# Hybrid decoder step: the sample columns' depthwise convolution moved from 31 small VectorE steps per tile to one GpSimd product and one VectorE sum

## The reference, cut to what matters

```
u = glu[..., :CONV_CH] * sigmoid(glu[..., CONV_CH:])
xx = concatenate([buf, u], 1)            # 30 old positions in front
y = dwconv_valid(xx, w) + b              # y[n] = sum_k w[k] * xx[n + k], k = 0..30
y = silu(layer_norm(y, ln_g, ln_b))
```

## Time and profile before

| | |
|---|---|
| median of 3 runs | 2254.72 us (2253.72 to 2254.95) |
| the profiled execution's own time | 2254.63 us |
| its span | 2252.8 us |
| TensorE matmul busy | 2067.1 us, 92% |
| VectorE busy | 1179.8 us, 52% |
| ScalarE busy | 388.3 us, 17% |
| GpSimd busy | 113.5 us, 5% |

### The profile page before, as it was taken

The page is one execution under the profiler, slowest core; times in us unless marked ns, Lnnn a source line. Parts: engine busy times, 40 slices in busy tenths (PEclk is TensorE's granted clock), DMA queues, the critical chain, the costliest instruction groups (busy, mean ns, idle before and its releaser), DMA issues.

```text
span 2252.8 us, 26851 instructions
## 1 busy us (share of the span) xinstructions
PE 2067.1 (92%) x9950; PEld 1581.3 (70%) x9950; DVE 1179.8 (52%) x3052; ACT 388.3 (17%) x1097; POOL 113.5 (5%) x219
## 2 busy tenths in 40 slices
PE   8998887897999999999999978769979999999999
PEld 6766655675777777777776666547757777777777
DVE  4998365445046776610059983654540567766000
ACT  1012266212110000000000132651120100000000
POOL 1002110000000000000000013000000000000000
PEclk9998688998999999999999986989989999999999
DMA  6103440573211222121231034015622122221121
GB/s 239 68 0 105 142 150 1 163 235 110 83 55 56 78 90 77 38 91 53 88 123 60 0 111 127 1 37 176 201 94 91 47 75 75 75 75 67 52 77 68
DMA packets 109988, 200.27 MB, mean 89 GB/s; under 512 B 13697, under 2 KB 81554, under 8 KB 104610
## 3 DMA queue, kind: packets, MB, share of 16 engines
q1 hardware_dynamic: 103618, 167.01, 22.3%
q0 software_dynamic: 5568, 30.38, 3.8%
q10 hardware_dynamic: 672, 1.16, 0.1%
HBM read 190.81 MB, written 15.94 MB: 92 GB/s over the span
## 4 chain that ended last, share of the span: by engine, by line
PE 84%; DVE 7%; ACT 6%; issue 1%; POOL 1%; DMA 1%; SPq 0%; DVEq 0%; ACTq 0%
PE ps L851 25%; PE ps L528 23%; PE ps L654 9%; PE ps L567 8%; PE ps L541 3%; PE ps L733 2%; PE ps L819 2%; PE ps L918 2%; PE ps L771 1%; ACT rC L1095 1%; ACT rA L1095 1%; PE ps L698 1%; PE ps L639 1%; PE ps L715 1%; ACT rB L951 1%; PE ps L519 1%
## 5 line engine op out<-in xcount | busy, mean ns | idle before, releaser
L528 PE MATMUL ps<-rC,rB 128*128 128x288 f32 x1232 | 300.1, 406 | 0.0
L528 PEld LDWEIGHTS ps<-rC,rB 128*128 128x128 f32 x1232 | 234.1, 190 | 64.7
L1665 DVE TENSOR_TENSOR xT<-xT,ps 128x576 f32<-128x576 f32 x16 | 12.1, 755 | 330.7 <-PE ps L528 294.0
L1294 DVE SCALAR_TENSOR_TENSOR catT<-XC,par,catT 128x512 f32<-128x512 f32 x240 | 180.4, 752 | 8.3
L851 PE MATMUL ps<-catT,rD 128*128 128x288 f32 x528 | 131.6, 406 | 0.0
L528 PE MATMUL ps<-catT,WR 128*128 128x288 f32 x512 | 130.0, 414 | 1.1 <-ACT catT L951 1.1
L654 PE MATMUL ps<-WR,rD 128*128 128x254 f32 x512 | 120.4, 393 | 0.0
L851 PE MATMUL ps<-catT,XC 128*128 128x288 f32 x480 | 119.8, 406 | 0.4 <-DVE rD L1621 0.4
L528 PEld LDWEIGHTS ps<-catT,WR 128*128 128x128 f32 x512 | 99.2, 194 | 29.4 <-ACT catT L951 1.5
L851 PEld LDWEIGHTS ps<-catT,rD 128*128 128x128 f32 x528 | 100.3, 190 | 27.7
L851 PE MATMUL ps<-rA,WR 128*128 128x288 f32 x448 | 117.8, 406 | 0.0
(11 more groups left out here) (287 smaller groups left out, 3199.9 us busy)
## 6 DMA issues: line engine op xcount, KB each, us to landing
WR<-in_w_up SPq DMA_DIRECT2D x56, 512.0 KB, 3.6
rB<-in_w_down SPq DMA_DIRECT2D x16, 1408.0 KB, 6.2
WR<-in_kvc SPq DMA_DIRECT2D x128, 128.0 KB
rB<-in_ksT SPq DMA_DIRECT2D x256, 64.0 KB, 1.9
rB<-in_w_up SPq DMA_DIRECT2D x32, 512.0 KB, 4.4
rD<-in_kvc SPq DMA_DIRECT2D x96, 128.0 KB, 2.3
WR<-in_w_glu SPq DMA_DIRECT2D x16, 512.0 KB, 5.3
WR<-in_w_out SPq DMA_DIRECT2D x16, 512.0 KB, 3.6
```

The costliest lines, as they stand in the source:

```text
L528: ins = mm(ps[:, bank + hf, 0:HN], w[:, k * P:(k + 1) * P], rhs[:, k, hf * HN:(hf + 1) * HN], start=k == 0, stop=k == K - 1)
L1294: stt(yc[:, 0:SEQ], xc[:, k:k + SEQ], w, yc[:, 0:SEQ], ALU.mult, ALU.add)
```

## The change

The sample columns leave the taps. GpSimd makes, for a whole tile, the products of all 31 taps: one multiply of 8 x 8 x 31 = 1984 elements per partition. Its first input is a view of `XC` in which rows overlap (step 1 for the position and step 1 for the tap), its second the 31 weights, broadcast over the 64 positions. VectorE then adds up the 31 products of each position with one reduce, and adds the bias with one more instruction. The products lie in `rC`, in three buffers `TM`; the fourth tile uses the first buffer again and waits for the first `conv_made`. The new semaphore is `tap_prod`. In a layer, GpSimd makes the four products ahead of its other work. Each prompt tap is now followed by `step` on itself, and the last one too.

```
+ TM = [rC[:, 5 * QKVC + DB * DS * CW * i:5 * QKVC + DB * DS * CW * (i + 1)] for i in range(3)]
+ def sample_products(c):                                      # GpSimd
+     xs = XC[:, c, XS0:XW]
+     taps = bass.AP(xs.tensor, xs.offset, [list(xs.ap[0]), [XSEG, DB], [1, DS], [1, CW]])
+     w = PV[:, 16 + 34 * c:16 + 34 * c + CW].unsqueeze(1).unsqueeze(1).to_broadcast([P, DB, DS, CW])
+     pool.wait_ge(*count("glu_done"))
+     if c >= 3:
+         pool.wait_ge(*count("conv_made"))
+     pool.tensor_tensor(TM[c % 3].rearrange("p (b n k) -> p b n k", b=DB, n=DS), taps, w, ALU.mult).then_inc(sh["tap_prod"], 1)
  def layer(l):                                                # GpSimd
+     pool.wait_ge(*count("par_in", 16))
+     pool.wait_ge(*count("hist_in", 16))
+     if l:
+         pool.wait_ge(sh["down_made"], l * KD)
+     for c in range(CT):
+         sample_products(c)
+     count("conv_made", 3)
...
  for k in range(first, last):                                 # VectorE, taps(c, first, last)
      if k == 0:
-         ts(yc[:, 0:SEQ], xc[:, 0:SEQ], w, bias, ALU.mult, ALU.add)
-         ins = ts(ys, xs[:, :, 0:DS], w, bias, ALU.mult, ALU.add)
+         ins = ts(yc[:, 0:SEQ], xc[:, 0:SEQ], w, bias, ALU.mult, ALU.add)
      else:
-         stt(yc[:, 0:SEQ], xc[:, k:k + SEQ], w, yc[:, 0:SEQ], ALU.mult, ALU.add)
-         ins = stt(ys, xs[:, :, k:k + DS], w, ys, ALU.mult, ALU.add)
+         ins = stt(yc[:, 0:SEQ], xc[:, k:k + SEQ], w, yc[:, 0:SEQ], ALU.mult, ALU.add)
      if k < CW - 1:
          step(ins)
  if last == CW:
-     ins.then_inc(sh["conv_made"], 1)
+     step(ins)
+     ys = yc[:, SEQ:NT]
+     dve.wait_ge(*count("tap_prod"))
+     step(dve.tensor_reduce(ys, TM[c % 3].rearrange("p (n k) -> p n k", k=CW), X, ALU.add))
+     bias = PV[:, 16 + 34 * c + CW:17 + 34 * c + CW]
+     ts(ys, ys, bias, None, ALU.add).then_inc(sh["conv_made"], 1)
```

## The result

The changed kernel takes 2267.23 us (median of 5 runs, 2265.29 to 2267.30) against 2254.72 before: 0.56% slower, ratio 1.0056, interval 1.0041 to 1.0070. In a later session, on another set of rounds, it took 2266.08 against 2254.70: ratio 1.0050, interval 1.0037 to 1.0063. The profiled execution is one of 2267.23 us with a span of 2265.5 us, 12.7 more than before.

A forecast was written before the change was run, and what follows sets the result against it. TensorE was taken to bound the convolution stretch up to ln_centre, with VectorE off the path. The forecast was 2254.63 + 9.0 us lateness + 3.4 us clock = 2267 us; likeliest case 2262 to 2274, whole range 2253 to 2273.

The forecast's parts named there:

- lateness: At glu(3), so the projection starts late: 4.5 us in each layer, 9.0 us in all.
- clock: TensorE at the projection's start: after 6.7 us idle the granted clock falls, losing 1.7 us per layer, 3.4 in all.
- Covers: VectorE's idle time before glu(1), glu(2), glu(3) if nothing else changed: 4.05, 3.17 and 0.91 us.
- The choice: do the taps stop?: VectorE's taps behind each glu: a GpSimd product stops them for as long as it reads, 4.2 us; chance 0.54.
- The power's row: GpSimd's power from 180.13 to 182.72, beside which two-input L1363 starts undelayed; taken as evidence against a standstill.
- P: Time for which one GpSimd product stops VectorE's taps, taken as 4.2 us.
- s1: Lateness at glu(1) in a layer: P - 4.05 = 0.15 us.
- s2: Lateness at glu(2) in a layer: s1 + P - 3.17 = 1.18 us.
- s3: Lateness at glu(3) in a layer: s2 + P - 0.91 = 4.47 us.
- no standstill: Rival: products read beside the taps, nothing late or gained, 2254.6 us (2253.6 to 2256); chance 0.30.
- mild: Rival: taps and product share the reads, taps lose half of P, 2.1 us; 2257 to 2260; chance 0.11.
- Faster: Rival: VectorE's taps delay TensorE's means in some executions, up to 8.3 us a layer returns; 2250 at best; chance 0.04.

The follow-up runs named there:

- e1: Changed kernel with GpSimd's products replaced by writes of zeros into the same 1984 columns: 2254.57 us, ratio 1.0000.
- e2: Changed kernel with GpSimd's products replaced by a one-input copy that does not read the weights: 2259.99 us, ratio 1.0027.
- e3: Kernel before, plus five extra VectorE instructions of the tap's form in front of glu(3) in each layer: 2267.25 us, ratio 1.0057.
- e4: Kernel before, plus two extra VectorE instructions of the tap's form in front of glu(3) in each layer: 2261.94 us, ratio 1.0040.
- e10: Changed kernel with the products made by VectorE instead of GpSimd, without an early start of the projection: 2254.67 us, ratio 1.0000.
- e5: Changed kernel with third product waiting for the last glu_done, sum of tile 0 behind glu(3), 13 taps of tile 1 before it: 2254.83 us, ratio 1.0014.
- e7: Changed kernel with TensorE starting the projection's first row tile without waiting for glu(3): 2248.39 us, ratio 0.9992.

## Why the prediction was right

It said 2267 and the time is 2267.2. The mechanism is the one forecast; that the number agrees to 0.2 us is luck. The terms were 9.0 us of lateness and 3.4 of clock, 12.4; measured are 6.5 and 5.2, 11.7, and 0.9 us more from stretches about which the prediction said nothing. Each step by itself:

- **Covers.** Forecast 4.05, 3.17 and 0.91 us with the products free. e1 shows 3.24 and 1.03 for the last two, and for the first 2.51 plus the 1.6 us for which its write held tap 0.
- **The sum.** Reduce 2.21, measured 2.22; bias 0.31, measured 0.25.
- **The product's length.** 4.2 us, measured 4.33 to 4.58. The Trainium skill's figure ("GPSIMD Engine Reference", 3.1 Elementwise) made it 4.36: the trace agrees, closer than my blend of rows.
- **The choice: do the taps stop?** Yes (e1, e2). The power's row, which spoke against it, is not refuted: it reads 14 elements. The rule of the Trainium skill ("SBUF — State Buffer", Who interferes with whom) is that a VectorE instruction with two SBUF inputs contends with a GpSimd one that reads SBUF, not with one that only writes it. The trace agrees: a tap of 4.5 us beside each product, 0.75 us beside the write. But VectorE does not lose the product's whole length, only 3.7 of 4.5 us.
- **Mis-sized: the lateness.** I took the stop to be as long as the product and put P at 4.2 us. The products are longer and the stop is shorter. With 3.7 my own sum gives s1 = 0, s2 = 0.53 and s3 = 0.53 + 3.7 - 0.91 = 3.32; the trace has 0.42 us of idle, then about 0.55 late, and 3.25. The total is 6.5 us and not 9.0, and TensorE idles 5.48 us where 6.7 were forecast.
- **Mis-sized: the clock.** I read 1.7 us per layer from one idle time of 3.79 us and used it for 6.7 us. After 5.4 and 5.5 us it is 2.62 to 2.75 (e3 and the changed kernel), after 2.7 and 3.0 it is 1.68 (e2, e4). The total is 5.2 us and not 3.4. "After the 2.23 us of now nothing falls" was true of the profile I had and not of every execution (e1).
- **Nothing gained.** Right: VectorE's spare time at `ln_centre` went from 0.53 to 8.12 us (5.9 of the 7.6 because TensorE's means come later). e10, with 4.69 us of it, and the second layer of e1, with 9.22, have the stretch of the kernel before to 0.01 us.

Of the rivals, "no standstill" falls by the 4506 ns tap and "mild" by its size. "Faster" falls by e1: VectorE was 9.2 us and more ahead of the means there, and nothing came back. What would have spared the chance of 0.30 for no change was not in the trace of before: it had no long GpSimd read beside a two-input instruction.

## What to carry to other kernels

Work moved from VectorE to an idle GpSimd is not gone from VectorE. Count for each moved instruction how long the other engine will be reading, and subtract that from the gain: here 120 short instructions (24 us per layer) became 10 us of sums and 15 us of standstill. That holds where VectorE's instructions read two tensors, as the taps do; the reduce was not held. Look next at where each standstill lands: the same four products cost 11.8 us in the changed kernel, and nothing in the stretch once the third stood behind `glu(3)` (e5) or TensorE no longer waited for `glu(3)` there (e7). And a gap on TensorE can cost more than its length, by the clock. Before shortening an engine that has slack, ask which wait makes the gap: here the moved wait and the shorter VectorE work were worth almost nothing each, and 2.35 to 2.49 us per layer together.

## What the runs showed of the hardware

- GpSimd at 1984 float32 elements: write 1.75 us, copy 2.14 to 2.34, product of two inputs 4.33 to 4.58. VectorE's product of the same views takes 2.22: against L1363's 0.75 us for 576 elements that is 1.04 ns an element, the same as the reduce's, so the overlapping rows and the broadcast cost nothing visible. GpSimd's first product and first copy, which start under VectorE's one-input tap 0, take 4.33 and 2.14 us; those that start under a two-input tap take 4.52 to 4.58 and 2.34.
- Beside the write, VectorE's TENSOR_SCALAR of 512 elements goes from 0.54 to 2.15 us while the two-input taps keep 0.75. Beside the product, a VectorE reduce of 1984 elements keeps 2.21 us and the TENSOR_SCALAR of 64 elements behind it takes 2.05 instead of 0.25; in the rows of e5 below, GpSimd's product starts at 88.18, and the 5.27 us of two taps hold the stop by the next one.

```profile
88.02 2.21 DVE L1318 TENSOR_REDUCE catT<-rC 128x64 f32<-128x1984 f32 x1
90.26 2.05 DVE L1320 TENSOR_SCALAR catT<-catT,par 128x64 f32<-128x64 f32 x1
92.23 5.27 DVE L1309 SCALAR_TENSOR_TENSOR catT<-XC,par,catT 128x512 f32<-128x512 f32 x2
```

- TensorE's granted clock after the same 2.22 us of idle stayed up in one layer of e1 (1.00) and fell in the other (0.57 in the window from 88 to 92).
